# The places of SBUF tiles in a single-core transformer-block kernel: bulk tiles moved to fixed offsets modulo 512 bytes

## The reference, cut to what matters

```
# first block
mod = silu(c) @ w_ada + b_ada                       # 1024 x 6144
h   = rms_norm(x, norm1_w) * (1 + sc1) + sh1
proj = h @ w_in                                     # 1024 x 2840
...  three-way attention (compressed, selected, window), short convolution, rms_norm
x = x + g1 * (mix @ w_out)
h2 = rms_norm(x, norm2_w) * (1 + sc2) + sh2
x = x + g2 * hier_moe(h2, ...)                      # 64 experts, top 2, w1, w3: 1024 x 512, w2: 512 x 1024
# second block, two layers
mod = silu(c) @ ada_w[l] + ada_b[l]                 # 1024 x 6144, for each of the 2 layers
layer 0: h = h + g1 * even_mixer(...)               # Fourier mix and window attention with a context
layer 1: h = h + g1 * pool_mix(...)
both:    h = h + g2 * (silu(hn @ w1) * (hn @ w3)) @ w2   # hidden width 2816
return rms_norm(h, final_g)
```

## Time and profile before

| | |
|---|---|
| median of three runs | 1794.41 us |
| the profiled execution, device time | 1793.89 us |
| its span, first to last instruction | 1792.1 us |
| mean granted TensorE clock | 0.882 of full |
| TensorE matmuls busy | 1398.0 us (78%) |
| VectorE busy | 611.7 us (34%) |
| ScalarE busy | 199.5 us (11%) |
| chain that ended last: DMA, TensorE, VectorE | 48%, 42%, 5% |
| bytes moved | 589.96 MB, mean 329 GB/s |

### The profile page before, as it was taken

One profiled execution on the slowest core, in us unless ns is written; L12 is line 12 of the kernel. 1 busy time (PEld: TensorE's weight loads), 2 busy tenths in 40 slices (PEclk: granted clock), 3 DMA queues, 4 the chain that ended last, 5 costly groups with the idle time before them and its releaser, 6 DMA issues.

```text
span 1792.1 us, 24506 instructions
## 1 busy us (share of the span) xinstructions
PE 1398.0 (78%) x10619; PEld 860.1 (48%) x10619; DVE 611.7 (34%) x956; ACT 199.5 (11%) x439; POOL 5.0 (0%) x10
## 2 busy tenths in 40 slices
PE   6978798675676666757676766666998999989997
PEld 4976755221222122212221122214886999879997
DVE  2654536200000000000000000006437777757785
ACT  2112322000000000000000000001332000120001
POOL 1000000000000000000000000000000000000000
PEclk8999999788888688888878798788999999989999
DMA  9789855999999999999999999995962654505541
GB/s 385 297 357 414 307 210 199 429 428 429 429 428 429 429 428 428 428 429 428 429 428 429 429 429 428 429 428 210 400 271 82 234 186 171 206 18 206 198 172 74
DMA packets 46260, 589.96 MB, mean 329 GB/s; under 512 B 5328, under 2 KB 7792, under 8 KB 9088
## 3 DMA queue, kind: packets, MB, share of 16 engines
q1 hardware_dynamic: 42464, 581.84, 78.7%
q10 hardware_dynamic: 3744, 7.37, 1.2%
HBM read 586.56 MB, written 2.62 MB: 329 GB/s over the span
## 4 chain that ended last, share of the span: by engine, by line
DMA 48%; PE 42%; DVE 5%; issue 2%; ACT 2%; SPq 0%; DVEq 0%; ACTq 0%
DMA ring<-in_w 44%; PE ps L1420 5%; PE ps L1842 4%; PE ps L1843 4%; PE ps L1847 4%; PE ps L1674 3%; PE ps L1581 3%; PE ps L1689 3%; PE ps L1364 2%; PE ps L1858 2%; PE ps L1861 2%; PE ps L1860 2%; DMA ring<-in_w_ada 1%; DVE ring_parts L747 1%; DMA ring<-in_mix_in 1%
## 5 line engine op out<-in xcount | busy, mean ns | idle before, releaser
L1674 PE MATMUL ps<-ring,mixT 128*32 128x512 f32 x2048 | 313.7, 749 | 178.9 <-DMA ring<-in_w 177.4
L1689 PE MATMUL ps<-ring,arena 128*32 128x512 f32 x1024 | 174.2, 818 | 105.7 <-DMA ring<-in_w 93.4
L1674 PEld LDWEIGHTS ps<-ring,mixT 128*32 128x32 f32 x2048 | 62.9, 123 | 401.7 <-DMA ring<-in_w 275.0
L747 DVE TENSOR_TENSOR ring_parts<-ring,ring_parts 128x1024 fp32r<-128x1024 f32 (+3 forms) x119 | 189.7, 1625 | 1.0
L1091 DVE TENSOR_TENSOR arena<-arena,ps 128x512 f32<-128x512 f32 x16 | 11.0, 688 | 512.7 <-PE ps L1674 512.5
L1842 PE MATMUL ps<-mixT_parts,ring_parts 128*128 128x256 f32 x704 | 168.0, 280 | 6.7 <-issue 6.7
L1843 PE MATMUL ps<-mixT_parts,ring_parts 128*128 128x256 f32 x704 | 167.5, 280 | 0.0
L1689 PEld LDWEIGHTS ps<-ring,arena 128*32 128x32 f32 x1024 | 33.6, 132 | 230.2 <-DMA ring<-in_w 144.3
L1842 PEld LDWEIGHTS ps<-mixT_parts,ring_parts 128*128 128x128 f32 x704 | 134.7, 191 | 8.0 <-issue 7.1
L744 DVE CAST ring_parts<-ring 128x1024 fp32r<-128x1024 f32 (+3 forms) x119 | 100.4, 891 | 105.3 <-DMA ring<-in_f 69.5
L1843 PEld LDWEIGHTS ps<-mixT_parts,ring_parts 128*128 128x128 f32 x704 | 134.7, 191 | 0.8
(11 more groups left out here) (342 smaller groups left out, 1381.1 us busy)
## 6 DMA issues: line engine op xcount, KB each, us to landing
ring<-in_w SPq DMA_DIRECT2D x192, 2048.0 KB, 26.0
ring<-in_ada_w SPq DMA_DIRECT2D x24, 2048.0 KB, 12.4
ring<-in_f SPq DMA_DIRECT2D x22, 2048.0 KB, 8.1
ring<-in_w_ada SPq DMA_DIRECT2D x12, 2048.0 KB, 13.7
ring<-in_f SPq DMA_DIRECT2D x22, 1024.0 KB, 6.4
ring<-in_w_in SPq DMA_DIRECT2D x5, 2048.0 KB, 14.4
ring<-in_w_out SPq DMA_DIRECT2D x2, 2048.0 KB, 9.8
ring<-in_mix_in SPq DMA_DIRECT2D x2, 2048.0 KB, 15.4
```

The source lines that it names most:

```text
L747: return tt(out.bitcast(F32R), v, hi, ALU.subtract)
L1674: last = mm(ps[rows[u], j, :], XeT[:, 2 * m + k, rows[u]], w[:, u, k * FE:(k + 1) * FE], start=(m == 0 and k == 0), stop=(m == 3 and k == 1))
L1689: last = mm(ps[rows[u], m, :], heT[:, k, rows[u]], w[:, u, m * 512:(m + 1) * 512], start=(k == 0), stop=(k == FE // P - 1))
```

## The change

Some tiles are allocated in another order, and two pads are put in so that bulk tiles start at chosen remainders of 512. `small` shrinks from 256 to 248 floats and `arena` from 11,400 to 11,136; both still hold all that is placed in them. No instruction, loop, semaphore or transfer is added, removed or moved: on each of the five engines the built program has the same instructions with the same waits in the same order, and only the addresses in them differ.

```
+SHIFT = 128
...
+        def onto(m):
+            at = nc.sbuf_base % 512
+            if at != m:
+                sb(f"pad{len(base)}", [P, (m - at) % 512 // 4])
...
-        ring = sb("ring", [P, NS, CHUNK])
         con = sb("con", [P, NCON])
         vec = sb("vec", [P, NVEC])
+        modcol = sb("modcol", [P, 3, 32])
+        ctxcol = sb("ctxcol", [P, 16])
+        small = sb("small", [P, 248])
+        brB = sb("brB", [P, 72])
+
+        cw2 = sb("cw2", [P, 2, 2, HD])
+        wr = sb("wr", [P, KD, 72])
+        onto(0)
+        ring = sb("ring", [P, NS, CHUNK])
+        modrow = sb("modrow", [P, 3 * 1536])
+        cond = sb("cond", [P, 2, KD, 32])
+        onto(SHIFT)
         x = sb("x", [P, NT, D])
         xn = sb("xn", [P, NT, D])
         hT = sb("hT", [P, KD, T])
         mixT = sb("mixT", [P, KD, T])
-        modrow = sb("modrow", [P, 3 * 1536])
-        modcol = sb("modcol", [P, 3, 32])
-        ctxcol = sb("ctxcol", [P, 16])
-        cond = sb("cond", [P, 2, KD, 32])
         gB = sb("gB", [P, D])
-        small = sb("small", [P, 256])
-        wr = sb("wr", [P, KD, 72])
-        brB = sb("brB", [P, 72])
         oh, relb = gB[0:NB, 0:384], gB[0:NB, 384:384 + NH]
-        cw2 = sb("cw2", [P, 2, 2, HD])
-        arena = sb("arena", [P, 11400])
+        arena = sb("arena", [P, 11136])
```

More of the change, by code:

```diff
@@ L133, in build @@
         mixT = sb("mixT", [P, KD, T])
-        modrow = sb("modrow", [P, 3 * 1536])
-        modcol = sb("modcol", [P, 3, 32])
-        ctxcol = sb("ctxcol", [P, 16])
-        cond = sb("cond", [P, 2, KD, 32])
         gB = sb("gB", [P, D])
-        small = sb("small", [P, 256])
-        wr = sb("wr", [P, KD, 72])
-        brB = sb("brB", [P, 72])
         oh, relb = gB[0:NB, 0:384], gB[0:NB, 384:384 + NH]
-        cw2 = sb("cw2", [P, 2, 2, HD])
-        arena = sb("arena", [P, 11400])
+        arena = sb("arena", [P, 11136])
         ringR, hTR, mixTR, arenaR = (parts(*a) for a in (
-            ("ring", [P, NS, CHUNK]), ("hT", [P, KD * T]), ("mixT", [P, KD * T]), ("arena", [P, 11400])))
+            ("ring", [P, NS, CHUNK]), ("hT", [P, KD * T]), ("mixT", [P, KD * T]), ("arena", [P, 11136])))
         ps = ctx.enter_context(nc.psum_tensor("ps", [P, 8, 512], F32))
@@ L175, in take @@
             at[0] += n
-            assert at[0] <= 11400, at[0]
+            assert at[0] <= 11136, at[0]
             return arena[:, at[0] - n:at[0]]
```

## The result

The changed kernel took 1797.46 us (median of 13 runs, 1792.42 to 1803.53), the kernel before on the same chip 1793.3 us (13 runs). The ratio is 1.0023, with a 95% interval of 1.0012 to 1.0033: slower by 0.23%, 4.2 us. The profiled execution took 1798.67 us with a span of 1796.9 us, 4.8 us longer than before.

What follows compares the result with a forecast made beforehand. The prediction took weight transfers to bound the expert stage and matmul start distances the feed-forward. Four TensorE terms summed to 7.2 us gained, everything else 0, giving 1787 us, with an 8-in-10 range of 1775 to 1802 us.

Steps and rivals of the forecast that it cites:

- What bounds the kernel: Expert stage bound by weight transfers, feed-forward by distances between matmul starts; transfers 44% of the chain, TensorE 42%.
- VectorE's 0: VectorE instructions: no change in cost from the new addresses, with bounds of 0.4 us either way.
- Term 3: Feed-forward first products: stationary pieces in one 512-byte block instead of two, 2112 x 1 ns = 2.1 us gained.
- one of its rivals: All TensorE loss was placement and may go in full: 19 us gained, 1775 us, chance 0.12.
- Term 1: Feed-forward second products: arena from 288 to 128 takes 234 to 229 ns, 528 x 4.6 ns = 2.4 us gained.
- Term 2: 512-column products, feed-forward and projections: moving ring rows touch four blocks, not five; 658 x 3.5 ns = 2.3 us gained.
- Term 4: Projections' 256-column products, some 430, half of them standing at 117 ns: 0.4 us gained.
- The slower rival: Feed-forward first products fall to the slow 117 ns pace: 7.6 to 10.5 us lost, say 1804 us, chance 0.20.
- Transfers: Expert weights' transfers into the ring: no change, with bounds of 1% or 9 us either way.
- its rival, at 1785 us: Expert transfers gain 1% or 9 us from the aligned ring, TensorE unchanged: 1785 us, chance 0.04.
- The sign that the prediction named for it, 432 GB/s: Expert stage at 432 GB/s or more, instead of 429, would show that transfers gained.
- Full relief: TensorE matmuls lose all placement cost: 19 us gained with the weight pace as floor, 1775 us, chance 0.12.

Runs made afterwards that it cites:

- experiment 2: Kernel after the change with the ring back at 128 and x, its relatives, gate row and arena at 128 too (remainders of 512): 1802.4 us.
- experiment 4: Kernel after the change with ring, x, its relatives, gate row and arena all at 0: 1794.7 us.
- experiment 7: Kernel after the change with ring at 0, x, its relatives and gate row at 192, arena at 0: 1787.6 us.
- experiment 8: Places of the kernel before (ring 128, x 320) with the arena alone moved from 288 to 128, in the new tile order: 1796.9 us.
- experiment 9: Two kernels made from the kernel after: ring 0, x 192, arena 160, 1786.8 us; and the remainders of before (128, 320, 288), 1793.1 us.
- Experiment 1: Remainders of the kernel before (x 320, arena 288) with the ring alone moved to 0: 1794.4 us.
- experiment 5: Three kernels from the kernel after, ring/x/arena: 256/448/256, 1787.9 us; 0/448/320, 1787.3 us; 64/320/320, time not given.
- experiment 3: Kernel after the change with ring at 0 and x, its relatives, gate row and arena at 192: 1785.4 us.

## Why the prediction was wrong

**What bounds the kernel: right.** The experts hang on transfers and the feed-forward on the distances between matmul starts, and both changed just where the stretches said they could. VectorE's 0 was right: 1220 ns on the splits of the ring before and after.

**Term 3, the first products: the step that failed.** The prediction put that their stationary pieces are 512 bytes long and "in the ring at 0 they lie in one block instead of two", 1 ns less for each, 2.1 us gained. Measured: 113.7 to 119.9 ns, 2112 x 6.2 = 13.1 us lost. The idea that failed is that a tile's own remainder makes a matmul fast or slow. With the ring at 0 the first products took anything from 113.7 to 120.0 ns, by where x was; with x at 320 they took 113.7, 117.8 or 119.9, by where the ring was (128, 0, 64); and experiments 2 and 4 have the same paces at different remainders. What counts first is the distance between the moving and the stationary start modulo 256, and for the first products the change moved it from 192, the best, to 128, one of the worst. At 192 the distance of the second products counts, too [experiments 7 to 9]. The prediction had the two numbers, "160 and 192 apart" before and "128 bytes apart" after, and used them only to judge one of its rivals.

Not all of the 13.1 us is in the stages: they grew by 9.3 us. The commonest step grew by 0.59 us, but the kernel before also had steps of 16.6 to 16.8 us, and over the 20 steps after a layer's first the mean went from 16.56 to 17.10 us, 20 x 0.54 = 10.9 us. The first steps went the other way: layer 1's from 19.65 to 18.32 us, since 26 first products of the kernel before ran at half the clock there and 12 of the kernel after, and layer 0's from 18.81 to 18.56 us. That leaves 9.3 us. An estimate of the change with equal clocks at that place is 1.3 us more, 10.6 us, from the 14 matmuls that ran at 0.21 instead of 0.12 us in the kernel before alone.

**Term 1, the arena: a size wrong, for the same reason.** 288 to 128 was to give 4.6 ns on 528 products, 2.4 us. It gave 0.9 ns, 0.5 us: the distance from ring to arena only went from 160 to 128. The same move with the ring left at 128 [experiment 8] made it 0 and gave 6.5 ns, so the 4.6 ns were no property of the arena's start. The 229 ns that the prediction saw in the projections were not due to a whole multiple of 64 but to a distance of 192; at distance 0 this shape takes 227 to 228 [experiments 2, 4, 8].

**Term 2, the ring's blocks: wrong.** It was to give 3.5 ns. Experiment 1 moved the ring to 0 and the second products went from 233.5 to 233.0 ns; experiments 2 and 4 have it at 128 and at 0 with 227.9 ns in both. In the projections with 512 columns the distance went from 192 to 128 and the pace from 229.5 to 232.4 ns.

**Term 4: wrong in sign.** Of the projections' 256-column products one group of 224 went from 282 to 292 ns mean duration, and its starts from 116 to 119 ns apart:

```profile
L1430 PE MATMUL ps<-mixT_parts,ring_parts 128*128 128x256 f32 x224 | 31.1, 292 | 5.4 <-DVE ring_parts L754 4.0 <-DVE ring_parts L757 1.5
```

That is one part of the 1.9 us of the first stage. Since that stage took 117.1 to 120.8 us in kernels with equal distances, no more is made of it.

**The slower rival: the right relation at another pace, with a chance of 0.20.** It named the relation between the ring as stationary and `mixT` as moving, and priced it at 7.6 to 10.5 us. The feed-forward and projections lost 11.2 us. But the first products did not fall into the slow pace of 117 ns that it had read; at a distance of 128 they stand at a third one, 119.9 ns. That its 1804 us is 6.5 us above the measured time is mostly the transfers' gain. The two paces, 113.6 and 117, that the prediction saw at one placement were real, too; they are the two rhythms, not a sign against places.

**Transfers: wrong, and this hid half of the loss.** The prediction took 0 and saw that rows of single transfers lean against a gain. A single transfer tells nothing here: the gain is 3.7 ns in 614.7 for each packet, 0.6%, 0.05 us in 8 us, below what those rows resolve. Over 925.9 us of stage it makes 5.6 us, and 5.8 us were measured. It lay within the bounds of 9 us, and its rival, at 1785 us, assumed that nothing happened on TensorE. The sign that the prediction named for it, 432 GB/s, was set just too high: 431 was measured.

The rule that the prediction quoted against its 0, from the Trainium skill, "DMA: Bandwidth & Descriptors", How a descriptor splits into AXI transactions, is borne out in its threshold: ring starts of 0 and 256 have 611.0 ns, those of 64 and 128 have 614.7 to 614.8. Its estimate of 0.8% is near the 0.6% measured. Two things don't fit: the Trainium skill tells it of bytes that are fetched, and here the place that is written to decides; and by an estimate from its beats a start at 64 should cost half as much as one at 128, while 614.8 and 614.7 ns were measured. And the rule of the Trainium skill that the prediction read as no effect at all, "SBUF — State Buffer", Who interferes with whom, with independent read ports for the moving operand and the weights, doesn't carry over to time here: the distance between the two tiles changed the pace by up to 6.6 ns in 113.4.

**Full relief: not met.** No placement brought the second products below 227.0 ns or the first below 113.4 on average. Plain passes stayed at 215 ns for 512 columns. The 216 ns that the Trainium skill gives for a single 512-column matmul by itself ("TensorE: Matmul & The Clock Gate", Back-to-back issue gap) were not reached by one-pass float32 matmuls anywhere here.

**The sum.** -5.8 (transfers) + 9.3 (feed-forward) + 1.9 (projections) - 0.6 (other stages) = +4.8 us of span; the medians say +4.2 us.

**What stays open.** Which part of the chip has the period of 256 bytes, and why second products at distance 0 bring the slow rhythm and those at 160 the fast one. At arena - ring = 64 and 192 [experiments 5 and 3] both rhythms came up within one run; how often each comes up in an unprofiled run was not measured. With x - ring at 192 the distance from arena to ring can't be told from that from arena to x, since the one fixes the other, so which of them chooses the rhythm is not shown. The first products were never seen at x - ring = 192 with arena - ring at 128 or 224. The growth of the first stage, 1.9 us, lies within what kernels with equal distances differ by.

## What to carry to other kernels

When a stage is bound by back-to-back matmuls, look at the distance between the starts of the stationary and the moving tile, modulo 256, before looking at either tile's own alignment; sweep it, since one pad costs less than 512 bytes of a partition and no time, and between the kernels before and after it was worth 0.6 us in a 17 us step. Where two kinds of such matmuls alternate, sweep both distances together. Place what large transfers fill at a multiple of 256 bytes. Price each with the stage's total, never with a single transfer or a single matmul, and change one tile at a time: moved together, a gain of 5.8 us and a loss of 11.2 us passed for one small loss.

## What the runs showed of the hardware that was not expected

- One-pass float32 matmuls with 256 moving columns started every 113.4 to 120.0 ns and those with 512 every 227.0 to 234.1 ns, at the full granted clock, depending on the distances between ring, x and arena. Plain float32 matmuls did not change with the places: two passes of 512 columns out of the ring (line 1581 of the kernel before) took 429.8 ns in every kernel.
- At a distance of 192 the 256-column matmuls keep one of two rhythms for a whole step, 113.4 or 117.8 ns, and the matmuls of another kind ahead of them decide which (60 of 60 steps fast at 160, 60 of 60 slow at 0). A tile that is no operand of a matmul can thus cost it 3.9 ns (experiment 8).
- Packets of 16,384 bytes into a ring at 0 or 256 took 611 ns, every one of some 18,430 between 400 and 1100 us; at 64 or 128 they took 611 to 626 ns, mean 614.6 to 614.8.
- After the same 3.33 us of idle time the granted clock of TensorE was 0.50 for 12 to 26 of the first matmuls of layer 1 in 13 of the 16 profiled executions, and 1.00 for all of them in three; that step was between 16.9 and 19.7 us long.
